# Hybrid decoder layer on one core: the output projection multiplied inside the last pair of heads, its low parts made on VectorE

## The reference

```
h = rmsnorm(x, attn_norm_w);  p = h @ w_in            # 1024 x 3328
o_da = diff_attention(rope(q), rope(k), v)            # 4 heads: two softmaxes, subtracted, rmsnorm
o_rw = rwkv7_group(p_rw, ...)                         # 8 heads of 64: a recurrence over the tokens, group norm, gate
x = x + concat(o_da, o_rw) @ w_out                    # 1024 x 1024: the output projection
h = rmsnorm(x, ffn_norm_w)
logits = h @ router_w + router_b                      # 32 experts
top_val, top_idx = top_k(logits, 4);  gates = softmax(top_val)
for each expert e, in blocks of rows that chose it:   # 32 experts, clamped SwiGLU
    gu = h[rows] @ mlp1_w[e] + mlp1_b[e]              # 1024 x 2048
    act = (up + 1) * gate * sigmoid(1.702 * gate)
    y = (act @ mlp2_w[e] + mlp2_b[e]) * gates         # 1024 x 1024, added to the rows
return rmsnorm(x + sum of y, final_norm_w)
```

## Time and profile before

| | us |
| --- | --- |
| runs | 1543.93, 1552.13, 1547.91 |
| profiled execution | 1548.19, of which its span is 1546.5 |
| busy PE, DVE, ACT, POOL | 1450.2, 1227.3, 1013.2, 458.8 |
| DMA traffic | 457.47 MB, mean 296 GB/s |
| output projection (L1387) in the chain of waits | 3% of the span |

### The profile page before, as it was taken

The page is one execution under the profiler, slowest core; times in us unless marked ns, Lnnn a source line. Parts: engine busy times, 40 slices in busy tenths (PEclk is TensorE's granted clock), DMA queues, the critical chain, the costliest instruction groups (busy, mean ns, idle before and its releaser), DMA issues.

```text
span 1546.5 us, 25543 instructions
## 1 busy us (share of the span) xinstructions
PE 1450.2 (94%) x9333; PEld 1071.9 (69%) x9334; DVE 1227.3 (79%) x1068; ACT 1013.2 (66%) x997; POOL 458.8 (30%) x253
## 2 busy tenths in 40 slices
PE   6999999996989999999999999999999999999884
PEld 5677777775867686777767677776777767656553
DVE  5565656565469799998989899889988989888984
ACT  4635353525256577776877878777777877677773
POOL 7200000000018431544425355322634525222210
PEclk9999999997979999999999999999999999999997
DMA  6211111004469899999999999999999999999992
GB/s 206 62 46 52 43 38 50 26 16 162 156 257 382 312 400 398 413 404 403 383 397 410 395 402 408 399 373 389 401 401 399 409 393 408 371 391 393 399 394 92
DMA packets 96941, 457.47 MB, mean 296 GB/s; under 512 B 11198, under 2 KB 37998, under 8 KB 47584
## 3 DMA queue, kind: packets, MB, share of 16 engines
q1 hardware_dynamic: 86176, 429.63, 69.5%
q0 software_dynamic: 10688, 26.80, 6.3%
HBM read 443.57 MB, written 18.10 MB: 299 GB/s over the span
## 4 chain that ended last, share of the span: by engine, by line
PE 38%; DMA 12%; DVE 10%; issue 9%; ACT 4%; POOL 2%; SPq 1%; DVEq 0%; ACTq 0%; POOLq 0%
DMA w_pieces<-in_mlp_w 10%; PE psum L2179 8%; PE psum L2200 5%; DVE w_pieces_lo L1943 5%; PE psum L2182 5%; PE psum L2250 4%; PE psum L2255 3%; PE psum L1387 3%; PE psum L2192 3%; PE psum L2189 3%; ACT w_pieces_hi L1743 3%; POOL slot_lists L1685 2%; DVE av L1968 1%; PE psum L2223 1%; DVE silu L1956 1%
## 5 line engine op out<-in xcount | busy, mean ns | idle before, releaser
L1943 DVE TENSOR_TENSOR w_pieces_lo<-w_pieces,w_pieces_hi 128x2048 fp32r<-128x2048 f32 x346 | 781.6, 2284 | 105.9 <-ACT w_pieces_hi L1743 104.3
L1743 ACT ACTIVATE w_pieces_hi<-w_pieces 128x2048 fp32r<-128x2048 f32 x346 | 660.8, 1915 | 245.7 <-DMA w_pieces<-in_mlp_w 174.4
L1676 POOL DMA_INDIRECT sum_rows<-ys,this_i x30 | 270.2, 9008 | 339.4 <-ACT ys L1795 196.6
L2250 PE MATMUL psum<-w_pieces_hi,ah 128*128 128x512 f32 x512 | 147.6, 392 | 7.0 <-DVE ah L1952 6.6
L2255 PE MATMUL psum<-w_pieces_lo,ah 128*128 128x512 f32 x512 | 139.9, 395 | 14.9 <-DVE w_pieces_lo L1943 14.8
L2200 PE MATMUL psum<-w_pieces,x_native 128*64 128x512 f32 x288 | 131.3, 598 | 0.0
L2189 PE MATMUL psum<-w_pieces_hi,xh 128*128 128x512 f32 x432 | 125.7, 414 | 2.9 <-ACT w_pieces_hi L1743 2.9
L2192 PE MATMUL psum<-w_pieces_lo,xh 128*128 128x512 f32 x432 | 119.3, 398 | 8.1 <-DVE w_pieces_lo L1943 8.1
L2255 PEld LDWEIGHTS psum<-w_pieces_lo,ah 128*128 128x128 f32 x512 | 95.3, 189 | 41.4 <-DVE w_pieces_lo L1943 22.4
L2179 PE MATMUL psum<-w_pieces_hi,xh 128*128 128x512 f32 x440 | 123.7, 403 | 0.0
L2182 PE MATMUL psum<-w_pieces_lo,xh 128*128 128x512 f32 x440 | 119.0, 392 | 1.1 <-DVE w_pieces_lo L1943 0.2
(11 more groups left out here) (421 smaller groups left out, 2233.3 us busy)
## 6 DMA issues: line engine op xcount, KB each, us to landing
w_pieces<-in_mlp_w SPq DMA_DIRECT2D x384, 1024.0 KB, 9.3
w_raw<-in_w_in SPq DMA_DIRECT2D x26, 512.0 KB, 4.0
w_pieces<-in_w_out SPq DMA_DIRECT2D x8, 512.0 KB, 9.3
chunk_work<-in_x SPq DMA_DIRECT2D x4, 512.0 KB, 6.6
sc<-pall POOLq DMA_DIRECT2D x16, 128.0 KB, 4.0
x<-in_x SPq DMA_DIRECT2D x4, 512.0 KB, 13.8
sum_rows<-x POOLq DMA_DIRECT2D x4, 512.0 KB, 3.2
h_rows<-w_pieces POOLq DMA_DIRECT2D x4, 512.0 KB, 2.9
```

Of the source, the lines that this page charges most:

```text
L1676: nc.gpsimd.indirect_dma_start(sum_dram, bass.IndirectOffsetOnAxis(this_i[rows, 0:1], 0), ys[rows, :], None, bounds_check=S - 1, oob_is_er ...
L1743: nc.scalar.activation(hi[:, p % RING], raw[:, raw_slot(b, p)].rearrange("p r n -> p (r n)"), ACT.Copy).then_inc(s_hi, done)
L1943: nc.vector.tensor_tensor(lo[:, p % RING], raw[:, raw_slot(b, p)].rearrange("p r n -> p (r n)"), hi[:, p % RING].bitcast(F32), ALU.subtrac ...
L2250: nc.tensor.matmul(bank(into + c), a[:, 2 * p + r2, :], hi[:, p % RING, r2 * D + c * 512:r2 * D + (c + 1) * 512], start=p == 0 and r2 == 0 ...
```

## The change

**Projection.** The eight parts of w_out are loaded by SP inside pair 3, in the order `OUT_ORDER` (attention heads and RWKV heads alternate), into the two buffers of the input weights. ACT rounds each (`split_out`) and each output tile (`raise_o`), DVE subtracts (`split_out`, `lower_o`); the low half of o is written over `o_t` itself. PE's `fold(count)` puts 26 of 48 fold steps, each of 3 matmuls, between the pair's work (4 + 4 + 2 + 2 + 3 up to the third weights' turn, then 1 six times, 3 and 2, at the places of `fill`): a step (f, i) multiplies o's part i, one of the first six, for the eighth f of the result. After y_sum come the 22 steps left, then parts 6 and 7. Four of the eighths are summed in two steps: `add_part` adds parts 0 to 5 into x, which is loaded again inside the pair, behind the third part of w_out. The four residual adds, squares and one root of four columns now end the first Block.

**Memory.** x lies in `x_home`, with `pall`, `cosb` and `sinb`; several buffers have two views. The halves of pieces (`hi`, `lo`) no longer share memory with what the routing uses. The router's weights are loaded at the start of the kernel.

**Second Block.** It has the transposes, then the logits, no projection. SP issues the bias loads and all six raw pieces with no wait. POOL stores the four tiles of x at once, then each h2 as it is ready. The low parts of the biases (three subtractions of 1024 columns) stand behind the keys on DVE; before they lay beside the projection. PE's first `up` waits for them.

```diff
+OUT_ORDER = (0, 4, 1, 5, 2, 6, 3, 7)
+READY = 6
+FOLD_ORDER = (4, 5, 6, 7, 0, 1, 2, 3)
+FINAL_BANKS = (4, 5, 2, 3, 6, 7, 0, 1)
...
+            if i < 2:
+                sp.wait_ge(s_wlo, IN_TILES + i - 1)
+            else:
+                sp.wait_ge(s_wout_lo[i - 2], 1)
+            sp.dma_start(w_out_raw(i), w_out_v[:, k, :]).then_inc(s_w[i % 2], 16)
+            if i == 2:
+                sp.wait_ge(PE.sem, PE.reached(HEADS - 1, "v_turn"))
+                sp.wait_ge(DV.sem, DV.reached(HEADS - 1, "ks"))
+                for t in (2, 3, 0, 1):
+                    sp.dma_start(x[:, t, :], x_v[:, t, :]).then_inc(s_xr, 16)
 
...
+        nc.gpsimd.dma_start(rwf[:], d["router_w"][0].rearrange("(p k) e -> p k e", p=P)).then_inc(s_router, 16)
+        nc.gpsimd.dma_start(rb[:], d["router_b"].to_broadcast([P, EXPERTS])).then_inc(s_router, 16)
+        nc.gpsimd.dma_start(scale[:], d["ffn_norm_w"].rearrange("a (p k) -> p (a k)", p=P)).then_inc(s_router, 16)
...
+        def split_out(i):
+            n = IN_TILES + i
+            act.wait_ge(s_w[n % 2], 16 * (n // 2 + 1))
+            if i < READY:
+                act.wait_ge(s_prod, min(n - 2, IN_TILES))
+            else:
+                act.wait_ge(PE.sem, PE.reached(HEADS - 1, "t_v"))
+                act.wait_ge(DV.sem, DV.reached(HEADS - 1, "bon"))
+            nc.scalar.activation(w_out_part(i, False), w_out_raw(i), ACT.Copy).then_inc(s_whi, 1)
+
+        def raise_o(i):
+            if i < READY:
+                act.wait_ge(DV.sem, DV.reached(HEADS - 2, "ot2"))
+            else:
+                act.wait_ge(DV.sem, DV.reached(HEADS - 1, "o_out" if i == READY else "ot2"))
+            nc.scalar.activation(o_hi[i], o_t[:, OUT_ORDER[i], :], ACT.Copy).then_inc(s_oh, 1)
...
                 split(n0 + 3)
+            else:
+                split_out(0)
+                raise_o(0)
+                raise_o(1)
+                split_out(1)
+                raise_o(2)
+                raise_o(3)
...
                 split(n0 + 5)
+            else:
+                split_out(3)
...
             output_copied(1)
+            if not more:
+                raise_o(4)
+                raise_o(5)
+                split_out(4)
...
                 copy_out(n0 + 5)
+            else:
+                split_out(7)
+                raise_o(6)
             act.wait_ge(PE.sem, PE.reached(j, "y_sum"))
             nc.scalar.activation(yr[:], bank(7), ACT.Ln, bias=con("gn_eps"), scale=1.0 / CH).then_inc(AC.sem, AC.step("y_log"))
             act.wait_ge(AC.sem, AC.reached(j, "y_log"))
             nc.scalar.activation(yr[:], yr[:], ACT.Exp, scale=-0.5).then_inc(AC.sem, AC.step("y_rs"))
+        raise_o(7)
+        for t in range(NT):
+            if t >= 2:
+                act.wait_ge(s_ss, t - 1)
+            act.wait_ge(s_x2, t + 1)
+            nc.scalar.activation(flat(w_raw[:, t % 2]), x[:, t, :], ACT.Square, accum_out=stat[:, 24 + t:25 + t]).then_inc(s_ss, 1)
+        act.wait_ge(s_ss, NT)
+        nc.scalar.activation(stat[:, 28:32], stat[:, 24:28], ACT.Sqrt, bias=con("eps"), scale=1.0 / D).then_inc(s_root, 1)
 
...
+        def split_out(i):
+            dve.wait_ge(s_whi, IN_TILES + i + 1)
+            nc.vector.tensor_tensor(w_out_part(i, True), w_out_raw(i), w_out_part(i, False).bitcast(F32), ALU.subtract).then_inc(s_wout_lo[i], 1)
+
+        def lower_o(i):
+            if not i:
+                dve.wait_ge(s_emptied, 16)
+            dve.wait_ge(s_oh, i + 1)
+            nc.vector.tensor_tensor(o_lo(i), o_t[:, OUT_ORDER[i], :], o_hi[i].bitcast(F32), ALU.subtract).then_inc(s_ol, 1)
+
+        def add_part(f):
+            t, c = divmod(FOLD_ORDER[f], 2)
+            dve.wait_ge(s_folded, f + 1)
+            dve.wait_ge(s_xr, 16 * NT)
+            part = x[:, t, c * 512:(c + 1) * 512]
+            nc.vector.tensor_tensor(part, bank(4 + f % 2), part, ALU.add).then_inc(s_fold, 1)
...
+            if not more:
+                lower_o(0)
+                lower_o(1)
+                split_out(1)
+                lower_o(2)
+                lower_o(3)
...
                 split(n0 + 5)
+            else:
+                lower_o(4)
+                lower_o(5)
+                split_out(4)
             largest(3)
             if more:
                 split(n0 + 6)
+            else:
+                split_out(5)
             weights(3)
+            if not more:
+                add_part(0)
+                add_part(1)
...
+        split_out(7)
+        lower_o(6)
+        dve.wait_ge(s_oh, KT)
+        nc.vector.tensor_tensor(o_lo(KT - 1), o_t[:, OUT_ORDER[KT - 1], :], o_hi[KT - 1].bitcast(F32), ALU.subtract).then_inc(s_ol_last, 1)
+        for t in range(NT):
+            dve.wait_ge(s_acc, t + 1)
+            first_bank = FINAL_BANKS[2 * t]
+            nc.vector.tensor_tensor(x[:, t, :], psum[:, first_bank:first_bank + 2, :].rearrange("p b n -> p (b n)"), x[:, t, :], ALU.add).then_inc(s_x2, 1)
 
...
+        def project_out(u, i, o, first, last):
+
+            t, c = divmod(u, 2)
+            for m, (a, w) in enumerate(((o_hi[i], w_out_part(i, False)), (o_hi[i], w_out_part(i, True)), (o_lo(i), w_out_part(i, False)))):
+                ins = nc.tensor.matmul(o, a[:, t * P:(t + 1) * P], w[:, c * 512:(c + 1) * 512], start=first and m == 0, stop=last and m == 2)
+            return ins
+
+        def fold_step(f, i):
+
+            if f == 0:
+                pe.wait_ge(s_wout_lo[i], 1)
+                pe.wait_ge(s_ol, i + 1)
+            if f == 1 and i == 0:
+                pe.wait_ge(AC.sem, AC.reached(HEADS - 1, "v_major"))
+            if f in (2, 3, 4, 5) and i == 0:
+                pe.wait_ge(s_fold, f - 1)
+            u = FOLD_ORDER[f]
+            ins = project_out(u, i, bank(4 + f % 2 if f < 4 else FINAL_BANKS[u]), i == 0, f < 4 and i == READY - 1)
+            if f < 4 and i == READY - 1:
+                ins.then_inc(s_folded, 1)
+
+        folds = iter([(f, i) for i in range(READY) for f in range(2)] + [(f, i) for f in range(2, KT) for i in range(READY)])
+
         for n in range(LEAD):
...
             fill(n0 + 3, 0, 2)
+            fold(4)
...
+            fold(2)
             ac("y_sq")
             nc.tensor.matmul(bank(7), con("heads"), ysq[:], start=True, stop=True).then_inc(PE.sem, PE.step("y_sum"))
+        for f, i in folds:
+            fold_step(f, i)
+        pe.wait_ge(s_wout_lo[6], 1)
+        pe.wait_ge(s_ol, READY + 1)
+        for u in range(4):
+            project_out(u, 6, bank(FINAL_BANKS[u]), False, False)
+        pe.wait_ge(DV.sem, DV.reached(HEADS - 1, "o_out"))
+        pe.wait_ge(AC.sem, AC.reached(HEADS - 1, "y_log"))
+        for u in (4, 5):
+            project_out(u, 6, bank(FINAL_BANKS[u]), True, False)
+        pe.wait_ge(DV.sem, DV.reached(HEADS - 1, "y_n"))
+        for u in (6, 7):
+            project_out(u, 6, bank(FINAL_BANKS[u]), True, False)
+        pe.wait_ge(s_wout_lo[7], 1)
+        pe.wait_ge(s_ol_last, 1)
+        for u in range(2 * NT):
+            last = project_out(u, 7, bank(FINAL_BANKS[u]), False, True)
+            if u % 2:
...
     def route_sync(sp):
-        for k in range(KT):
-            sp.dma_start(wo[:, k, :], w_v[:, k, :]).then_inc(s_w[k], 16)
-        for t in range(NT):
-            sp.dma_start(x[:, t, :], d["x"][0, t * P:(t + 1) * P, :]).then_inc(s_xr, 16)
         for n in range(4):
             sp.dma_start(bias_raw[32 * n:32 * n + 32, :], d["mlp1_b"][0][:, (n // 2) * D:(n // 2 + 1) * D]).then_inc(s_bl, 16)
 
         for n in range(4):
             sp.dma_start(down_raw[32 * n:32 * n + 32, :], d["mlp2_b"][0]).then_inc(s_dl, 16)
 
-        sp.wait_ge(s_bias, 3)
         for p in range(RAW):
-            if p == 1:
-                sp.wait_ge(s_store, 16 * NT)
-                sp.wait_ge(s_log, NT)
-            if p == 3:
-                sp.wait_ge(g["s_gath"], 16)
             sp.dma_start(raw[:, p].rearrange("p r n -> p (r n)"), gate_up_rows(d, 0, p)).then_inc(g["s_raw"][p], 16)
...
         for t in range(NT):
-            if t == NT - 1:
-                pool.wait_ge(s_acc, NT)
-                g["zero_rows"]()
-            pool.wait_ge(s_x2, t + 1)
             nc.gpsimd.dma_start(g["sum_dram"][t * P:(t + 1) * P, :], x[:, t, :]).then_inc(g["s_kept"], 16)
+        for t in range(NT):
             pool.wait_ge(s_h2, t + 1)
             nc.gpsimd.dma_start(g["h2_dram"][t * P:(t + 1) * P, :], h2[:, t, :]).then_inc(s_store, 16)
+        pool.wait_ge(s_log, NT)
+        g["zero_rows"]()
         pool.wait_ge(s_store, 16 * NT)
...
+        def copied(t):
+            act.wait_ge(s_turn, t + 1)
+            nc.scalar.activation(x2t[:, :, t * P:(t + 1) * P], flat(t).rearrange("p (k c) -> p k c", c=P), ACT.Copy).then_inc(s_xt[t], 1)
+
+        nc.scalar.activation(stat[:, 52:53], con("eps"), ACT.Exp)
+        copied(0)
+        copied(2)
...
+        def copied(t):
+            dve.wait_ge(s_turn, t + 1)
```

(31 more changed lines are left out.)

## The result

The changed kernel takes 1569.29 us (median of 4 runs, 1563.77 to 1572.23), the kernel before 1549.72 beside it: ratio 1.0128, 95% interval 1.0086 to 1.0169. It is slower by some 20 us, where 1545.0 was forecast and 1535 to 1557 given as the range. The profiled execution took 1572.23 us (span 1570.6), that of before 1548.19. The time of one kernel spreads over some 10 us between executions, so a trace is read for the length of its parts, and the medians for the whole.

A forecast was written before the change was run, and what follows sets the result against it. It took the wait chain ahead of the DMA-bound experts as movable: pair end, last projection matmul, mask, lists. A 21 us projection gain, mostly repaid, left lists 3 earlier: 1548.19 - 3 = 1545.2, forecast 1545.0, range 1535 to 1557.

The forecast's parts named there:

- The mechanism of the gain: Output projection after y_sum: moved matmuls and removed idle, slow-clock and routing stretches save 38 us, 21 net of the lengthened pair.
- Both new waits on PE: Last pair, fold steps i=4 and i=5: PE waits for DVE's low parts and splits, 2.0 and 2.5 us.
- Station 1, the last pair: End of the last pair of heads: y_sum at 381.4 instead of 364.28, 17 us later.
- By the pair before: Last pair sized from the preceding pair's 80.2 us plus 1.4 for six more matmuls: 81.6, y_sum at 375.1.
- DVE's delay: Last pair: new low parts and a split ahead of ek and the softmax maximum, 4.0 us, of which 1.8 remains.
- Rival (d): Last pair longer still: each moved split delays DVE's chain in full, 12.3 us more, 6 counted; 1551 us, chance 0.08.
- Station 4, mask to gather: Mask to lists: late biases cost 2.5 to 3 us, some 2 of the 4.9 gain left; lists 3 earlier.
- It is the larger of the two, not their sum: Between mask and first expert: POOL's store-and-gather path and DVE's path run side by side; the longer one counts.
- rival (c): Last h2 store and gather meet six piece loads and four x stores: store 16.3 us, +13.3, 1558 us; chance 0.13.
- 6 MB are through in 16 us: Second block: the six piece loads start 18.7 us before the last h2 store, so they should be finished by then.
- After that nothing is changed: From the lists to the kernel's end: no change in time, put at nothing.
- Rival (a): Expert weight stream: three pieces of 2.63 us loaded ahead pay in full, 7.9 us earlier, 1537 us; chance 0.18.

The follow-up runs named there:

- the better places: Changed kernel with the four fold steps of parts 4 and 5 moved from ahead of akv to behind the products before the chunks: 1559.43 us, ratio 1.0078.

## Why the prediction was wrong

**Right.** The mechanism of the gain: behind y_sum the projection and the routing to the mask take 50.1 us instead of 71.2; 49.1 was forecast. The last add, square, root and barrier came to 4.5 (415.03 to 419.53), as forecast; ffn_norm_w landed in 7.2 (6.9 taken), and the mask came 18.1 after the Block's start (18.7). The last projection matmul ended 27.5 behind y_sum, 25.9 forecast, at the full clock: a matmul took 0.233 us and not 0.227. Both new waits on PE were there, 1.96 and 2.45 us long and on DVE (2.0 and 2.5 forecast).

**Station 1, the last pair: mis-sized.** 17.1 us more were forecast, 22.2 more it was (92.99 for 70.8). Two terms of the sum failed. "By the pair before" gave 10.8 for the matmuls with all splits; they came to 13.6 at the better places (4.8 and 8.8), for the splits cost something of their own. The two new waits, with 1.8 of DVE's delay, were put at 6.3; their lengths were right, but with what stands behind them on PE (5.9) and the clock (2.7) they cost 8.6. In all the pair hid 0 to 3 of 17.7 at the changed kernel's places, where the forecast let it hide 6.9. Rival (d), a longer pair by 6, came true in its size, not in its reason: the splits cost 4.8 together at most and not 12.

**Station 4, mask to gather: the wrong case.** "It is the larger of the two, not their sum" was right; but I let the last h2 store take 2.9 or 6.9, and it took 15.53. This was rival (c), with a chance of 0.13, priced by the reload's 16.3, right to 0.8 us; of its price of 13.3 on the forecast 10.6 came true. "6 MB are through in 16 us" was the argument against it, and it left out what else was asked for by then: 2 MB of x, 2 of h2, 1 of biases, 0.5 of ffn_norm_w. That is 12.1 MB, of which 0.9 had moved by 425; the other 11.2 at 425 GB/s are 26 us, to 451, and the store landed at 453.24. The traces with one early piece gave 3.2 to 5.1 us, that with two 6.5, with three 8.0, and with six 13.5 to 17.2 (10.3 without the x stores ahead).

By the Trainium skill ("DMA: Bandwidth & Descriptors", section "Queues, rings and completion order") the engines go round between the queue rows. The trace agrees: 193 packets of SP's queue and 189 of POOL's from 430 to 435. In the prediction I read from it that the store is quick. But its row gets only a third of the bytes beside SP's, and the last h2 store has four x stores, ffn_norm_w and three h2 stores of its own row ahead of it. From 437.71 on POOL's row had 1.9 MB left to move, 13.7 us at 0.139 MB a us; 15.53 it was. With six pieces both rows end together, so the sum of all bytes gives nearly the same; which of the two holds with more pieces than six was not tried.

**Behind the lists: no step at all.** "After that nothing is changed" held for the program. The time from the first sum to the end, put at nothing, was 9.4 longer, in the first traces all of it behind the 25th gather. The buffers had moved, and the same move in the kernel before gave about half of it there; the rest stays open. Even a sum right in all its other steps would have missed the traced time by as much.

**Rival (a)**, the head start of the stream, is refuted: the head start brought nothing (the fourth gather 14.6 later than before), and giving it up cost nothing (fourth gather at 522.67). That the six buffers hold no more than six pieces either way is the likely reason, argued and not tested.

## What to carry to other kernels

Price a transfer on the critical path by the bytes asked for before it on every queue; prefetches issued "for nothing" beside it are paid there (3.2 us became 15.5 here). Work put into another stage's gaps is cheap only where an engine was idle before and the operands are ready: two waits of 2 us on PE cost 6 to 9. When an edit changes the size of an early allocation, run the kernel before with the same shift, and compare stretch by stretch: two sums that agree can be made at different places. And before two traces are compared at a station, take off what they differ by at the station before.

## What was not expected of the hardware

1216 bytes a partition of unused SBUF ahead of the streamed buffers made 1022 to 1023 us of experts 1029 us long, and with 2048 bytes they took 1022 (1.0031 with 1.0012 to 1.0049, and 1.0007 with 0.9990 to 1.0023). Which buffer and which access it is wasn't tried.

With SP's and POOL's queue both full each moved about as many packets (1298 and 1296 from 419 to 453.3), and so 7.75 MB against 4.72, for POOL's packets are the smaller ones.

Of the same program with the same two waits on PE, of 1.96 and 2.45 us, one execution kept the granted clock at 1.00, and in five others it fell behind them, to 0.51 to 0.70 in windows of 3 us: 90.3 us for the pair against 92.8 to 93.3. The pair of the kernel before shows both as well: 0.50 from 358 to 361 in the first trace, 1.00 in the second, and 70.8 against 69.8 us.
